# Numbering the tokens of the biased heads by column in a diffusion-transformer block

## What is computed

```python
def _na_pattern(rows):
    kh = min(NA_MAX_KH, rows)                       # 8 of 16 rows
    ...
    rs = row_start(q_r)                             # clip(r - 4, 0, 8)
    cs = np.clip(q_c - NA_KW // 2, 0, GRID_W - NA_KW)   # 16 of 64 columns
    row_ok = (k_r[:, None, :] >= rs[:, :, None]) & (k_r[:, None, :] < rs[:, :, None] + kh)
    col_ok = (k_c[None] >= cs[:, None]) & (k_c[None] < cs[:, None] + NA_KW)
...
s_loc = jnp.einsum('bnqhd,bnjhd->bnhqj', qb, kg).astype(jnp.float32) * scale + bias
s_loc = jnp.where(jnp.asarray(mask)[:, None], s_loc, -jnp.inf)
s_ctx = jnp.einsum('bnqhd,bjhd->bnhqj', qb, k_ctx).astype(jnp.float32) * scale
p = jax.nn.softmax(jnp.concatenate([s_loc, s_ctx], axis=-1), axis=-1)
```

## Time and profile before

| | |
|---|---|
| median of three runs | 2657.88 us (2656.96 to 2660.88) |
| span of the profiled execution | 2660.7 us |
| mean granted TensorE clock | 0.992 |
| TensorE busy | 2584.3 us (97%) |
| VectorE busy | 1469.8 us (55%) |
| ScalarE busy | 1041.6 us (39%) |
| GpSimd busy | 1149.2 us (43%) |

### The profile page before, as it was taken

One profiled execution on the slowest core, in us unless ns is written; L12 is line 12 of the kernel. 1 busy time (PEld: TensorE's weight loads), 2 busy tenths in 40 slices (PEclk: granted clock), 3 DMA queues, 4 the chain that ended last, 5 costly groups with the idle time before them and its releaser, 6 DMA issues.

```text
span 2660.7 us, 33072 instructions
## 1 busy us (share of the span) xinstructions
PE 2584.3 (97%) x12561; PEld 2088.5 (78%) x12561; DVE 1469.8 (55%) x1880; ACT 1041.6 (39%) x1715; POOL 1149.2 (43%) x689
## 2 busy tenths in 40 slices
PE   7999999999999999999999999999998999999997
PEld 5778799998878888888886777667877888887885
DVE  4673289998267665654334111224179788776333
ACT  4651467887254233221113441224244444441113
POOL 0224223563375555555445211113475555555452
PEclk9999999999999999999999999999999999999998
DMA  7462110333312322234322111001512222235321
GB/s 287 128 209 68 23 41 18 74 77 115 102 64 79 119 72 95 80 127 131 99 80 96 40 32 40 24 25 40 166 48 70 74 95 80 72 113 191 99 79 63
DMA packets 71581, 235.12 MB, mean 88 GB/s; under 512 B 8945, under 2 KB 11121, under 8 KB 71298
## 3 DMA queue, kind: packets, MB, share of 16 engines
q1 hardware_dynamic: 71426, 233.02, 26.7%
HBM read 179.77 MB, written 39.85 MB: 83 GB/s over the span
## 4 chain that ended last, share of the span: by engine, by line
PE 81%; DVE 13%; issue 3%; ACT 2%; DMA 1%; POOL 0%; SPq 0%; DVEq 0%; ACTq 0%
PE S L863 17%; PE S L463 11%; PE S L464 11%; PE S L841 9%; PE S L845 9%; PE S L842 9%; PE M L948 2%; PE S L697 1%; DVE pt L1710 1%; DVE S L1691 1%; PE M L713 1%; DVE xt L1806 1%; PE M L466 1%; PE S L963 1%; PE S L482 1%
## 5 line engine op out<-in xcount | busy, mean ns | idle before, releaser
L2188 POOL TENSOR_TENSOR wbl<-rf,wbh 128x512 fp32r<-128x512 f32 (+1 forms) x352 | 513.0, 1463 | 478.4 <-ACT wbh L1258 478.3
L1258 ACT ACTIVATE wbh<-rf 128x512 fp32r<-128x512 f32 (+1 forms) x352 | 215.1, 620 | 691.1 <-PE S L863 366.8
L2065 POOL TENSOR_TENSOR wl<-raw,wh 128x1024 fp32r<-128x1024 f32 x59 | 147.1, 2495 | 579.4 <-ACT wh L1018 579.4
L841 PE MATMUL S<-th_t,wbh 128*128 128x512 f32 x640 | 253.0, 395 | 6.4 <-POOL wbl L2188 3.6
L845 PE MATMUL S<-tl_t,wbh 128*128 128x512 f32 x640 | 252.3, 394 | 0.0
L842 PE MATMUL S<-th_t,wbl 128*128 128x512 f32 x640 | 251.7, 393 | 0.0
L863 PE MATMUL S<-fh,wbh 128*128 128x512 f32 x704 | 221.1, 393 | 2.6 <-DVE xt L1758 2.6
L863 PE MATMUL S<-fl,wbh 128*128 128x512 f32 x704 | 220.0, 392 | 1.3 <-POOL fl L2212 1.3
L863 PE MATMUL S<-fh,wbl 128*128 128x512 f32 x704 | 220.2, 392 | 0.0
L463 PE MATMUL S<-hh,wh 128*128 128x512 f32 (+1 forms) x456 | 193.9, 425 | 10.9 <-DVE gt L1994 3.1
L841 PE MATMUL S<-th_b,wbh 128*128 128x512 f32 x480 | 189.3, 394 | 0.7 <-ACT ub L1363 0.4
(11 more groups left out here) (348 smaller groups left out, 5784.4 us busy)
## 6 DMA issues: line engine op xcount, KB each, us to landing
ff<-hid SPq DMA_DIRECT2D x44, 512.0 KB, 6.2
rf<-in_w_d SPq DMA_DIRECT2D x80, 256.0 KB, 2.7
mr<-in_w_modT SPq DMA_DIRECT2D x32, 512.0 KB, 4.9
rf<-in_w_f1g SPq DMA_DIRECT2D x22, 512.0 KB, 3.8
rf<-in_w_f1u SPq DMA_DIRECT2D x22, 512.0 KB, 3.4
hid<-pr SPq DMA_DIRECT2D x22, 512.0 KB, 2.6
rf<-in_w_f2g SPq DMA_DIRECT2D x22, 512.0 KB, 5.3
rf<-in_w_f2u SPq DMA_DIRECT2D x22, 512.0 KB, 3.6
```

The lines of the kernel that those rows point to most:

```text
L841: e.matmul(o, hi[:, k, :], th[part][:, k, :], start=k == 0, stop=False)
L1258: e.activation(flat(wbh[wslot(f, n)][:, :, :])[:, 0:x.shape[1]], x, ACT.Copy).then_inc(*w_hi.mark((f, n)))
L2065: e.tensor_tensor(l, raw[:, w % 3, 0:n], h.bitcast(F), ALU.subtract).then_inc(*w_lo.mark(w))
L2188: e.tensor_tensor(l, x, h.bitcast(F), ALU.subtract).then_inc(*w_lo.mark((f, n)))
```

## The change

The tokens of the b heads are numbered by column of the grid: place 16 c + r instead of 64 r + c. A block of 128 queries is then 8 columns with all 16 rows. Its queries see up to 8 columns to the left and 7 to the right, so the keys are the block itself and its two neighbours, 384 columns, or 256 for the first and the last block. The items of the b heads get the same `k0` and `L` as those of the a heads. The bias table has three parts (inner block, first, last), 384 + 256 + 256 = 896 columns.

The new order arises where VectorE copies the projection units of the b heads out of PSUM (`by_column`, four keys, four queries, four value units). It is undone where the outputs are turned back, for tiles 4 to 7: `token_order` and `as_turned` give the views with which ScalarE and VectorE write `hh` and `hl`. A half of a turned tile is then 32 columns of all rows instead of 512 consecutive tokens. The padding columns of `pp`, their memset and TensorE's wait for it go away; an item with 256 local keys has two pairs of score matmuls and four tiles in one bank.

```diff
-B_START = [0, 0, 0, 128, 256, 384, 512, 512]
-B_SIZE = [512, 512, 576, 576, 576, 576, 512, 512]
-B_COL = [6 * 64, 4 * 64, 896, 896, 896, 896, 2 * 64, 0]
+NBIAS = 384 + 256 + 256
+B_COL = [384] + 6 * [0] + [640]
 ITEMS = []
 for _n, (_kind, _h, _p) in enumerate(HEADS):
     for _b in range(8):
-        if _kind == "a":
-            _b0, _b1 = max(_b - 1, 0), min(_b + 1, 7)
-            ITEMS.append((_n, _kind, _h, _p, _b, 128 * _b0, 128 * (_b1 - _b0 + 1)))
-        else:
-            ITEMS.append((_n, _kind, _h, _p, _b, B_START[_b], B_SIZE[_b]))
+        _b0, _b1 = max(_b - 1, 0), min(_b + 1, 7)
+        ITEMS.append((_n, _kind, _h, _p, _b, 128 * _b0, 128 * (_b1 - _b0 + 1)))
...
-    bt = [at(f"bt{z}", a, [128, 1472], F) for z, a in enumerate([AH + 46 * KB, AH + 52 * KB])]
+    bt = [at(f"bt{z}", a, [128, NBIAS], F) for z, a in enumerate([AH + 46 * KB, AH + 52 * KB])]
...
+    def by_column(x):
+
+        return x.rearrange("p (c r) -> p r c", r=16)
+
+    def by_row(x):
+        return x.rearrange("p (r c) -> p r c", c=64)
+
+    def columns_of(x, half):
+
+        return x.rearrange("p (r h c) -> p h c r", h=2, c=32)[:, half]
...
+        def as_turned(k, half):
+
+            x = turned_out(k, half)
+            return x if k < 4 else x.rearrange("p (c r) -> p c r", r=16)
+
+        def token_order(x, k, half):
+
+            return x[:, HALF[half]] if k < 4 else columns_of(x, half)
...
-                    parts += [(256, 512, k0, None), (512, w, k0 + 256, None)]
+                    parts.append((256, 512, k0, None))
+                    if L > 256:
+                        parts.append((512, w, k0 + 256, None))
...
-                        e.wait_ge(*d_set("pad"))
...
-                    e.activation(hh[:, k, HALF[half]], turned_out(k, half), ACT.Copy, scale=g).then_inc(*a_hh.mark(("out", k, half)))
+                    e.activation(token_order(hh[:, k, :], k, half), as_turned(k, half), ACT.Copy, scale=g).then_inc(*a_hh.mark(("out", k, half)))
...
-                e.tensor_copy(d[:, 0:1024], S[SL.of[u]][:, :]).then_inc(*d_ev.mark(u))
+                if rope or (kind == "v" and m == 0):
+                    e.tensor_copy(d[:, 0:1024], S[SL.of[u]][:, :]).then_inc(*d_ev.mark(u))
+                else:
+                    e.tensor_copy(by_column(d[:, 0:1024]), by_row(S[SL.of[u]][:, :])).then_inc(*d_ev.mark(u))
...
-                    if i == 0:
-                        e.memset(pp[:, :, 832:896], 0.0).then_inc(*d_set.mark("pad"))
...
-                for half, r in enumerate(HALF):
+                for half in range(2):
                     e.wait_ge(*a_hh(("out", k, half)))
-                    e.scalar_tensor_tensor(hl[:, k, r], turned_out(k, half), g, hh[:, k, r].bitcast(F),
+                    e.scalar_tensor_tensor(token_order(hl[:, k, :], k, half), as_turned(k, half), g,
+                                           token_order(hh[:, k, :].bitcast(F), k, half),
                                            ALU.mult, ALU.subtract).then_inc(*d_hl.mark(("out", k, half)))
```

More of the change, by code:

```diff
@@ L2584, in bias_index @@
 def bias_index():
-    dr = np.zeros((128, 23, 64), int)
-    dc = np.zeros((128, 23, 64), int)
-    ok = np.zeros((128, 23, 64), bool)
-    q = np.arange(128)
-    qr, qc = q // 64, q % 64
-    kc = np.arange(64)
-    c0 = np.clip(qc - 8, 0, 48)
-    col_ok = (kc[None] >= c0[:, None]) & (kc[None] < c0[:, None] + 16)
-    es = list(range(1, 15)) + list(range(3, 12))
-    for s, e in enumerate(es):
-        dr[:, s, :] = np.clip(e - qr, 0, 14)[:, None]
-        dc[:, s, :] = np.clip(kc[None] - qc[:, None] + 15, 0, 30)
-        row = np.ones(128, bool)
-        if s >= 14 and e == 3:
-            row = qr == 0
-        if s >= 14 and e == 11:
-            row = qr == 1
-        ok[:, s, :] = col_ok & row[:, None]
-    return dr.reshape(128, -1), dc.reshape(128, -1), ok.reshape(128, -1)
+    q, k = np.arange(128), np.arange(384)
+    qc, qr = q // 16, q % 16
+    r0 = np.clip(qr - 4, 0, 8)
+    drs, dcs, oks = [], [], []
+    for q0, k0, n in ((8, 0, 384), (0, 0, 256), (56, 48, 256)):
+        kc, kr = k0 + k[:n] // 16, k[:n] % 16
+        c0 = np.clip(q0 + qc - 8, 0, 48)
+        row_ok = (kr[None] >= r0[:, None]) & (kr[None] < r0[:, None] + 8)
+        col_ok = (kc[None] >= c0[:, None]) & (kc[None] < c0[:, None] + 16)
+        drs.append(np.clip(kr[None] - qr[:, None] + 7, 0, 14))
+        dcs.append(np.clip(kc[None] - q0 - qc[:, None] + 15, 0, 30))
+        oks.append(row_ok & col_ok)
+    return np.concatenate(drs, 1), np.concatenate(dcs, 1), np.concatenate(oks, 1)
 def cols(v):
```

## The result

The kernel after takes 2638.15 us, the median of four runs (2637.46 to 2641.76), beside 2658.26 for the kernel before on the same chip. The ratio is 0.9929, with an interval of 0.9915 to 0.9943: 15 to 23 us less, where 27.6 were predicted. The sign is right. The medians differ by 20.1 us (the ratio gives 18.9), so some 7.5 us of the forecast saving are missing.

What follows compares the result with a forecast made beforehand. VectorE was taken to bound the b heads, before and after. Eight heads at 3.6 us less (-28.8), +1.2 for nearly equal engines, +0.5 squares, -0.5 drain and 0 for strided writes gave -27.6: 2630.3 us, range 2627 to 2639.

Steps and rivals of the forecast that it cites:

- favoured case: Whole kernel: VectorE sets the pace and strided writes are free; 2630.3 us, by itself 2627 to 2634, chance 0.60.
- the term of 0.5 us for side work: b heads: ScalarE's squares in eight items exceed VectorE's time per item, adding 0.5 us or so once.
- VectorE's own work in a head goes from 20.05 to 16.45: b heads: shorter bias pass (1.6 us) and low parts (2.0 us) take 3.6 us off VectorE's work per head.
- The drain: Behind the last item: fewer transposes and weighings and no second ScalarE copy, by estimate 0.5 us less.
- I charge 0.15 us a head for what two nearly equal engines cost each other: b heads: with TensorE only 4% under VectorE, 0.15 us a head is added, 1.2 over eight heads.
- the rival of the a heads' pace: b heads fall to the a heads' 17.57 us a head and no further, saving 20.3: 2637.6 us, chance 0.15.
- eight items also carry a square of 0.63 ... 0.5 us or so once: b heads: in eight items ScalarE takes 2.2 us against VectorE's 2.06, costing 0.5 us or so once.
- I take nothing, since the row at 0.41 us is the same engine with a still longer step: Copies of projection units and turned output tiles: strided SBUF writes cost 0, judged by a strided PSUM read.
- the bound of 2.3: Strided SBUF writes: at most 2.3 times a column, from GpSimd's two-operand pass against a cast.
- the bound of 7.4: Start of attention and output turn: 7.4 us more in all if strided writes cost 2.3 times.
- the strided rival: Strided writes to SBUF cost: 2637.7 us at the bound, 2634 at half of it, chance 0.20.

Runs made afterwards that it cites:

- e12: Kernel after with the five tiles of a b item's transposed weights divided 3 + 2 between the two PSUM banks instead of 4 + 1: 2638.46 us.
- e6: Kernel after with VectorE's low part of the first bank written for two of four tiles only, in b items from 68 on: 2632.04 us, one run.
- e7: Kernel after with one idle matmul of 256 columns added ahead of the scores of each b item: 2637.32 us, one run.
- e10: e9 plus the b heads' minimum in one biased pass over context and local keys, separate context reduction removed, context scores with opposite sign: 2630.99 us.
- e11: Kernel after with only the b heads' minimum in one biased pass, separate context reduction removed, context scores with opposite sign: 2635.47 us.
- e2: Kernel after with idle matmuls ahead of the scores of items 80 (14), 99 (14) and 100 (5): 2638.48 us.
- e3: Kernel after with squares, logarithm, exponential and last normalization cut to 8 columns, so those norms are not computed: 2634.58 us.
- e8: Kernel before with squares, logarithm, exponential and last normalization cut to 8 columns, so those norms are not computed: 2655.22 us, one run.
- e1: Kernel after with the same reordering, but SBUF writes run on and the large steps lie on the PSUM reads: 2637.31 us.
- e9: Kernel after with normalization moved from item 98 to 103, large steps on PSUM reads, idle matmuls at item 80 and more in the drain: 2632.03 us.
- e13: Kernel after with tiles divided 3 + 2 between the banks and the b heads' minimum in one pass, sign right: 2628.36 us.
- e14: Kernel after with 3 + 2 tiles in all heads, one-pass minimum, strides on PSUM reads, late normalization, idle matmuls at item 80 and behind last join: 2620.08 us.
- e5: Kernel after with strides on PSUM reads, squares in every second item, last exponential and normalization in four pieces, idle matmuls at items 68, 88, 89: 2638.80 us.
- e4: Kernel before with only the change's column-major copies and reordered writes of turned tiles 4 to 7 added: 2661.27 us.

## Why the prediction was right in sign and 7.5 us too low

The favoured case had two halves: VectorE sets the pace, which held, and strided writes are free, which didn't; its own 2627 to 2634 us missed. The largest error is in neither half but in the term of 0.5 us for side work. The steps that failed, in the prediction's words:

**Right: what bounds and what goes.** The step "VectorE's own work in a head goes from 20.05 to 16.45" held: e12, which shortens the bank loop, runs at 16.47. The bias pass took 0.49 us for 256 columns, as predicted. VectorE stayed the bound (e6 and e7: less work on it gave time, more on TensorE took almost none). The drain gave 0.46, predicted 0.5.

**Off by 0.9: "I charge 0.15 us a head for what two nearly equal engines cost each other".** It was 0.26 (16.71 less 16.45), 0.11 more over eight heads. What it pays for was named wrongly. It is not TensorE, which took one more matmul per item for 0.05 a head, but the bank loop, which the rival of the a heads' pace had named: the 3 + 2 cut gave 0.24 of the 0.26 back. As a rival that one was wrong: the b heads run at 16.7 and not at 17.57. But the loop is why e10 and e11 gave so little at the steady pace.

**Off by 4.5: "eight items also carry a square of 0.63 ... 0.5 us or so once".** This is the largest piece. Above the steady pace lay 5.5 us before and 10.6 after, 5.0 more against 0.5. The step looked at the squares alone. Each interval less the steady one at the same place of a head, summed by items (rounding makes 5.4 and 10.5 of the two sums):

| us above the steady pace | hand-over, 64-69 | squares, 70-78 | logarithm, table loads, 79-83 | exponential, 84-97 | normalization, 98-103 | sum |
|---|---|---|---|---|---|---|
| before | 0.8 | 0.0 | 2.6 | 0.2 | 1.8 | 5.4 |
| after | 1.6 | 0.9 | 4.0 | 0.5 | 3.5 | 10.5 |
| e2, clock kept up | 1.6 | 0.9 | 2.8 | 0.5 | 2.3 | 8.0 |
| e3, thin | 1.6 | 0.0 | 2.1 | 0.0 | 1.2 | 4.8 |
| e8, before, thin | 0.8 | 0.0 | 1.8 | 0.0 | 0.8 | 3.4 |

The squares grew by 0.9 where 0.5 was priced. All other columns were priced at nothing. Between before and after two things add up. The clock's two falls are 2.5 (after less e2, all in the columns of the logarithm and the normalization). The other 2.6 (e2 less before) is work that lay partly in the slack of a 20 us head: squares 0.9, hand-over 0.8, normalization 0.5, exponential 0.3, table loads 0.1. (0.5 of the hand-over isn't slack: before, the first two b intervals were that much shorter than the steady ones, with the low parts of 0.88 and 0.69 us of the earlier trace rows in them, and after they aren't.) The thin side work kept the clock up too (1.00 in 508 to 516 us of e3), so its 5.6 contain the clock's share and the two aren't added. How far the two falls are owed to the change stays open: the stalls of TensorE are longer than before (2.15 and 1.93 against 1.69 and 1.72 us), but in e6 the clock stayed at 1.00 behind one of 2.16.

**Off by 3: "I take nothing, since the row at 0.41 us is the same engine with a still longer step".** The row was of a strided read from PSUM, and the new pattern a strided write to SBUF; e1 shows that these are not alike. The factor is 1.5 to 1.6, within the bound of 2.3. By stages it costs 0.6 us at the start and 2.4 to 2.6 in the turn. At (1.6 - 1) / (2.3 - 1) of the bound of 7.4 the rival would have given 3.4, and 3.0 to 3.2 came. The pair of before and after shows only 1.0 of the turn, because before had a fall of the clock there.

**The count.** Predicted -27.6. Pace +0.9, above the pace +4.5, and about +0.5 for an interval that I counted both in the eight heads and in the drain: -21.7, as measured in b heads and drain (-21.24 - 0.46). Start +0.6, turn +1.0, a heads -0.3: -20.4, beside -20.1 of the medians.

In the end the strided rival (chance 0.20) and an unpriced side cost held at once. The range reached to 2639 for the rivals one by one; that the median of 2638.15 lies close below its end is luck, since nothing at that end of the range stood for a side cost above 0.5 us or for the clock. The ratio applied to the shown median of 2657.88 gives 2639.01, at its very end.

The Trainium skill, "Advanced Engine Details and Errata", section Memory Cachelines, had said that accesses to SBUF each on another 16-byte line pay a penalty. The runs agree: steps of 64 bytes cost VectorE 1.6 times and steps of 256 bytes cost both engines 1.5 to 1.6 times. On PSUM the section says that access which isn't contiguous slows matmuls; e1's reads of PSUM by VectorE and ScalarE, at steps of 256 and 64 bytes, cost nothing.

## What to carry to other kernels

When a stage gets faster, price again all that was done beside it: what lay in the slack of the old pace is on the path of the new one. Where TensorE stalls amid dense work, read the granted clock behind the stall: here it stayed or fell, and a fall cost 1.2 to 1.7 us. Before a stage's time is put down to an edit, look whether the clock fell in one of the two profiles and not in the other. When a copy must permute, let the read from PSUM jump and the write to SBUF run on. When removing work from the bound gives almost nothing at the steady pace, look for a second limit of the same length: two edits worth 0.2 us a head each were worth 1.3 together.

## What the runs showed of the hardware

- A write to SBUF at steps of 64 bytes takes VectorE 1.6 times a plain one (1.95 against 1.22 us), one at steps of 256 bytes takes ScalarE 1.6 times (1.083 against 0.685) and VectorE 1.5 times (1.134 against 0.743; this one reads an SBUF operand at the same steps, and the two aren't told apart). A read from PSUM at such steps costs nothing (1.216, 0.685 and 0.743 in e1).
- A VectorE instruction with two SBUF operands takes longer when it meets certain passes of GpSimd: 2.47 and 1.54 us instead of 0.48 for 256 columns, 2.33 instead of 1.30 for 1024. The Trainium skill, "GPSIMD Engine Reference", section 1. Specifications, says that the two engines share their SBUF interfaces; the traces agree. Each ended shortly after GpSimd's pass did, and the later the more columns it had: 0.03 us for 8 columns, 0.28 for 256 (twice), 1.09 for 1024 (1.08 in before). That looks as if it had been held until the pass ended and had only then run; GpSimd's next cast then took 2.25 us instead of 1.25 in after. A cast held it as well: the sum of four numbers in the hand-over took 1.08 us and ended 0.01 us after the cast. GpSimd's scaling of one tensor beside it in e9 did not (1.30 us).
- A stall of TensorE was followed by a granted clock of 0.50 in some executions and not in others, at almost the same length. It fell behind 2.15 and 1.93 us in after and 1.83 in e1. It stayed at 1.00 behind 1.69 and 1.72 in before, 1.82 in after, 2.16 in e6 and 2.27 in e12. At item 80, behind 2.15 to 2.17 us without idle matmuls, it fell in five of six kernels (after, e1, e11, e12 and e13, not e6); with fourteen idle matmuls there it fell in none of four (e2, e9, e10, e14). At the output turn it fell in before, e2, e3, e5 to e8 and e11, and not in after, e1, e4, e9, e10 and e12 to e14. A fall costs 1.4 to 1.7 us there, which is why single medians here tell less than the stages.
